# The bias rows leave SBUF once and are spread from memory to memory later

## The chip, the cores and the metric

The kernel runs on one core of one Trainium2 chip. The metric is the device time of one execution in microseconds; the time given is the median of several runs.

## The reference

Two blocks follow each other on one activation `x` of 256 tokens by 1024 channels, all float32. The first mixes with a gated linear recurrence and a 16-head forgetting attention, and has a gated feed-forward part. The second has two layers with SwiGLU parts, of which the last mixes with an 8-head attention (called "moba"). Only that attention uses the relative-position bias, a table of 32 buckets by 8 heads that is looked up by the distance of query and key:

```python
dist_own = qpos[:, None] - (j * MOBA_BLOCK + jnp.arange(MOBA_BLOCK))[None, :]
bias_own = rel_table[t5_bucket(dist_own)].transpose(2, 0, 1).astype(f32)
s_own = jnp.einsum('bhqd,bhpd->bhqp', qb, kown).astype(f32) * scale + bias_own
s_own = jnp.where(dist_own >= 0, s_own, -jnp.inf)
```

For one head the bias depends on the distance alone. So one row of 384 numbers (`EXT`) holds all that a head needs, and query p reads the same row, shifted by p places.

## The kernel before

**The stream of weights.** All weights are one stream of parts, each 128 x 1024 float32 (512 KB), in the order of the phases in `PHASES`: `xa`, `v`, `gates`, `ga`, `qk`, `sa`, `sb`, `pa`, `pb`, `wo` and so on. SyncE loads part c into `raw[c % 4]` as soon as VectorE has made `w_lo` of part c-4 (function `load`). ScalarE makes the rounded half `w_hi` (`hi`, four parts ahead of TensorE), VectorE the remainder `w_lo` (`lo`, three parts ahead), and TensorE multiplies each part as three products of 128 x 128 by 256 columns per block (L1291, L1292, L1293, or L1384 to L1386 for token tiles). A full part has eight blocks, 24 matmuls. Each engine runs its own list in program order; semaphores alone tie them.

**Phases around the change.** `v` (8 parts, token tiles; ScalarE evacuates in pairs in `token_pair`, L356) is followed by `gates`, the two sigmoid gates of the recurrence: 8 parts that hold 8 and 5 blocks in turn, 156 matmuls in all. Their weights are parts 18 to 25. ScalarE writes the gates with a sigmoid (L375) out of banks 4 to 7, and between two evacuations of `v` it does the exponentials and the logarithms of the forget gate (`exponentials`, `logarithms`), each with a table load. After `ga` come `qk`, `sa`, `sb`; at their end POOL multiplies the last product of the recurrence (L1185) and has then nothing to do until the `merged` tiles are complete (L1187), where it loads `x` again and the level masks.

**The bias rows.** TensorE makes `ext`, 8 rows of 384 (one a head, on partitions 0 to 7), early in the program. ScalarE copies them to SBUF, in `work` where the sigmoids later write. POOL sends them to the memory tensor `bias_rows`, 128 copies a head (L1155), and ScalarE waits for the end of that transfer, semaphore `ext_out` (named bias_rows_out), before its first sigmoid:

```python
act.wait_ge(ext_out, 16)
for n in range(8):
    multiplied(PART["gates"] + n)
```

Much later, behind the SwiGLU loop of the first layer, POOL reads them back with a step of 383 per partition (L1271), which gives each partition its shift; VectorE adds the mask to them.

Of the kernel before, what the change touches and what calls it, by code (L numbers as in the profile page):

```python
# [13 lines left out]
F32 = mybir.dt.float32  # L14
# [6 lines left out]
P = 128  # L21
# [7 lines left out]
H_MOBA, DH_MOBA = 8, 128  # L29
# [37 lines left out]
EXT = 3 * P  # L67
# [4 lines left out]

def build(nc, stream, par_d, x_d, wf_d, table_d, onehot_d, ident_d, mask_d, lmask_d, out_d):
    scr = nc.dram_tensor("bias_rows", [H_MOBA, P, EXT], F32, kind="Internal")
    with ExitStack() as ctx:
        def sb(name, shape, dt=F32):
            return ctx.enter_context(nc.sbuf_tensor(name, shape, dt))

        def sem(name):
            return ctx.enter_context(nc.semaphore(name))  # L80
# [22 lines left out]
        def flat(ap):  # L103

            return ap.rearrange("p u t -> p (u t)")
# [7 lines left out]
        ext = flat(F[0:H_MOBA, 60:62, :])[:, 0:EXT]  # L113
# [30 lines left out]
        def dcol(name, e):  # L144
# [11 lines left out]
        x_in = [sem(f"x_half_in{i}") for i in range(2)]  # L156
        par_in, wf_in, tab_in, cst_in, x_back, lm_in, bias_in = (
            sem(n) for n in ("par_in", "wf_in", "table_in", "const_in", "x_back", "lmask_in", "bias_in"))
        ext_out, out_done = sem("bias_rows_out"), sem("out_done")
        ones_ready = sem("ones_ready")  # L160
        sq_ready, stat_done, rms_ready, rstd_ready = (
            sem(n) for n in ("square_ready", "stat_done", "rms_ready", "rstd_ready"))
# [93 lines left out]
        def _(act):  # L256
# [104 lines left out]
            for n in range(0, C, 2):  # L361
# [3 lines left out]
                if n == 4:  # L365
                    logarithms()
                    A(touch, touch, ACT.Sigmoid)
            act.wait_ge(ext_out, 16)
            for n in range(8):
                multiplied(PART["gates"] + n)  # L370
                m, g = n // 4, n // 2 % 2
# [150 lines left out]
            for l in range(1, LEVELS + 1):  # L522
                e, n = EB[l % 2], 2 * (l - 1)
# [604 lines left out]
        def _(pool):  # L1128
# [20 lines left out]
            for t in range(R):  # L1149
# [2 lines left out]
                                ALU.subtract).then_inc(xcl_ready, 1)  # L1152
            pool.wait_ge(ext_ready, 1)

            pool.dma_start(bass.AP(tensor=scr, offset=0, ap=[[P * EXT, H_MOBA], [EXT, P], [1, EXT]]),  # L1155
                           ext.rearrange("h (o e) -> h o e", o=1).to_broadcast([H_MOBA, P, EXT])).then_inc(ext_out, 16)

            pool.wait_ge(cst_in, 32)
            g.tensor_copy(EYE_R, ident[0:H_FOX, 0:H_FOX]).then_inc(cum_split, 1)
# [19 lines left out]
            for t in range(R + 2):  # L1179
                if t < R:  # L1180
                    g.tensor_tensor(IG[:, t, :], IG[:, t, :], XC[:, t, :], ALU.mult).then_inc(b_done, 1)
                if t >= 2:
                    pool.wait_ge(scan_done, t - 1)
                    pool.wait_ge(gelu_done, 1)
                    g.tensor_tensor(GA[:, t - 2, :], GA[:, t - 2, :], XC[:, t - 2, :], ALU.mult).then_inc(ya_done, 1)  # L1185

            pool.wait_ge(merged, C)  # L1187
            pool.dma_start(X, x_d).then_inc(x_back, 16)
            pool.dma_start(LM, lmask_d).then_inc(lm_in, 16)
# [80 lines left out]
            for j, (a, e) in enumerate([(0, P), (P, EXT)]):  # L1270
                pool.dma_start(BIAS[:, :, a:e], bass.AP(tensor=scr, offset=255 - P * j,  # L1271
                               ap=[[EXT - 1, P], [P * EXT, H_MOBA], [1, e - a]])).then_inc(bias_in, 16)
# [495 lines left out]
```

## Time and profile before

| | |
|---|---|
| median of 3 runs | 1272.76 us (1271.36 to 1272.99) |
| the profiled execution's span | 1272.8 us |
| TensorE busy | 1222.9 us, 96% |
| VectorE, ScalarE, POOL busy | 69%, 53%, 33% |
| mean granted TensorE clock | 0.974 |
| slices with a granted clock of 0.7 | one, the third of 40 (64 to 95 us) |

The profiled execution has its own time, which is its span, 1272.8 us, and lies at the median of the runs. How to read it: TensorE has work for nearly the whole span, so what counts is where it stands still or runs at a lowered clock. The page's 40 slices show one place where the clock fell to 0.7, in the third slice, and it is there that one reads on.

### The profile page before, as it was taken

To read this page: it belongs to the slowest core of one execution; us is meant where nothing else is said; L and a number is where in the kernel's file an instruction comes from. 1 tells how busy PE (TensorE), PEld (TensorE's weight loads), DVE (VectorE), ACT (ScalarE), POOL (GpSimd) and SP (SyncE) were. 2 spreads that over 40 slices of the span, in tenths; PEclk is the share of its full clock that TensorE was granted. 3 is DMA by queue.
4 is the path that set the end of the run, shared out by engine and by line. 5 is a ranking of instruction groups with operands and counts; after the bars stand their busy time and mean duration, and the time that the engine had idled before them with its cause. 6 is when DMAs were issued, how large, how long until landed. Compare 5 with 4: busy or idle time off the path is not lost.

```text
span 1272.8 us, 26105 instructions
## 1 busy us (share of the span) xinstructions
PE 1222.9 (96%) x9746; PEld 1194.9 (94%) x9746; DVE 876.0 (69%) x1215; ACT 680.4 (53%) x1017; POOL 425.8 (33%) x425
## 2 busy tenths in 40 slices
PE   8959999999999999999989989999999999999997
PEld 8949988899989999998989989999999999999996
DVE  7817666596789999547878778555666777655653
ACT  6538744563557677445634345555445555555542
POOL 3206200060235555212055547444321005544421
PEclk9979999999999999999988889999999999999999
DMA  6556522356635655652623325565765545655662
GB/s 220 157 132 219 157 95 83 103 153 209 230 91 181 191 172 187 206 180 86 201 78 100 100 67 169 181 183 183 250 206 168 182 134 150 190 186 178 194 202 76
DMA packets 56535, 204.51 MB, mean 161 GB/s; under 512 B 6616, under 2 KB 6744, under 8 KB 56336
## 3 DMA queue, kind: packets, MB, share of 16 engines
q1 hardware_dynamic: 54288, 197.35, 49.7%
q0 software_dynamic: 1600, 5.10, 1.9%
q8 instruction: 52, 0.85, 0.3%
q10 hardware_dynamic: 576, 1.05, 0.2%
q14 instruction: 19, 0.16, 0.0%
HBM read 200.85 MB, written 2.62 MB: 160 GB/s over the span
## 4 chain that ended last, share of the span: by engine, by line
PE 84%; DVE 9%; DMA 3%; ACT 2%; issue 1%; DVEq 0%; SPq 0%; ACTq 0%
PE bank L1291 25%; PE bank L1292 24%; PE bank L1293 24%; DMA raw<-in_stream 3%; DVE w_lo L642 2%; PE bank L1546 2%; PE bank L1473 1%; PE bank L1384 1%; PE bank L1385 1%; PE bank L1386 1%; DVE work L982 1%; DVE h_lo L672 1%; DVE work L796 1%; PE bank L1475 1%; DVE work L696 1%
## 5 line engine op out<-in xcount | busy, mean ns | idle before, releaser
L642 DVE TENSOR_TENSOR w_lo<-raw,w_hi 128x1024 fp32r<-128x1024 f32 x374 | 489.3, 1317 | 181.4 <-ACT w_hi L265 180.5
L1291 PE MATMUL bank<-h_hi,w_hi 128*128 128x256 f32 x1888 | 543.8, 288 | 9.5 <-DVE h_lo L672 5.2
L1292 PE MATMUL bank<-h_lo,w_hi 128*128 128x256 f32 x1888 | 536.6, 284 | 0.0
L1293 PE MATMUL bank<-h_hi,w_lo 128*128 128x256 f32 x1888 | 536.4, 284 | 0.0
L265 ACT ACTIVATE w_hi<-raw 128x1024 fp32r<-128x1024 f32 x374 | 392.1, 1052 | 242.1 <-PE bank L1293 218.6
L1291 PEld LDWEIGHTS bank<-h_hi,w_hi 128*128 128x128 f32 x1888 | 364.7, 193 | 16.2 <-issue 7.6
L1292 PEld LDWEIGHTS bank<-h_lo,w_hi 128*128 128x128 f32 x1888 | 365.0, 193 | 0.3
L1293 PEld LDWEIGHTS bank<-h_hi,w_lo 128*128 128x128 f32 x1888 | 364.6, 193 | 0.0
L1291 PE MATMUL bank<-u_hi,w_hi 128*128 128x256 f32 x868 | 250.3, 288 | 19.1 <-DVE w_lo L642 13.2
L1292 PE MATMUL bank<-u_lo,w_hi 128*128 128x256 f32 x868 | 248.6, 286 | 0.0
L1293 PE MATMUL bank<-u_hi,w_lo 128*128 128x256 f32 x868 | 248.4, 286 | 0.0
L1291 PEld LDWEIGHTS bank<-u_hi,w_hi 128*128 128x128 f32 x868 | 169.5, 195 | 21.3 <-issue 11.1
L678 DVE TENSOR_TENSOR work<-bank,work 128x256 f32<-128x256 f32 x218 | 90.5, 420 | 123.4 <-PE bank L1293 119.3
L1292 PEld LDWEIGHTS bank<-u_lo,w_hi 128*128 128x128 f32 x868 | 169.7, 196 | 0.0
L1293 PEld LDWEIGHTS bank<-u_hi,w_lo 128*128 128x128 f32 x868 | 169.7, 195 | 0.0
L1220 POOL TENSOR_TENSOR work<-work 128x256 f32<-128x256 f32 x68 | 82.4, 1211 | 177.6 <-ACT work L569 118.9
L1203 POOL TENSOR_TENSOR work<-work 128x256 f32<-128x256 f32 x46 | 34.5, 750 | 135.3 <-DVE work L1056 79.6
L1225 POOL TENSOR_TENSOR u_lo<-work,u_hi 128x256 f32 x68 | 70.1, 1031 | 11.4 <-POOL u_hi L1223 11.4
L569 ACT ACTIVATE work<-work 128x256 f32<-128x256 f32 x44 | 18.4, 417 | 74.1 <-PE bank L1293 74.1
L1384 PE MATMUL bank<-w_hi,h_hi 128*128 128x256 f32 x192 | 56.9, 296 | 0.0
L1385 PE MATMUL bank<-w_hi,h_lo 128*128 128x256 f32 x192 | 56.1, 292 | 0.0
L1386 PE MATMUL bank<-w_lo,h_hi 128*128 128x256 f32 x192 | 55.9, 291 | 0.0
(223 smaller groups left out, 1299.7 us busy)
## 6 DMA issues: line engine op xcount, KB each, us to landing
raw<-in_stream SPq DMA_DIRECT2D x374, 512.0 KB, 3.7
bias_rows<-work POOLq DMA_DIRECT2D x1, 1536.0 KB, 35.5
work<-in_x_t SPq DMA_DIRECT2D x2, 512.0 KB, 6.3
work<-in_x_t POOLq DMA_DIRECT2D x1, 1024.0 KB, 6.6
work<-bias_rows POOLq DMA_DIRECT2D x1, 1024.0 KB, 10.9
out<-work ACTq DMA_DIRECT2D x4, 256.0 KB, 2.5
work<-in_lmask POOLq DMA_DIRECT2D x1, 512.0 KB, 7.9
work<-bias_rows POOLq DMA_DIRECT2D x1, 512.0 KB, 6.5
```

What stands on the lines that cost most here:

```text
L265: A(w_hi[:, slot, :], raw[:, slot, :], ACT.Copy).then_inc(hi_ready, 1)
L642: v.tensor_tensor(w_lo[:, slot, :], raw[:, slot, :], w_hi[:, slot, :].bitcast(F32), ALU.subtract).then_inc(lo_ready, 1)
L678: v.tensor_tensor(dst, out_of(t), RSTD, ALU.mult).then_inc(evacuated, 1)
L1203: chain.wait(g.tensor_tensor(SQT, src[:, c, :], src[:, c, :], ALU.mult))
L1220: g.tensor_tensor(PB[:, pair, :], GB[:, pair, :], YB[:, 2 * pair + 1, :], ALU.mult).then_inc(pair_free, 1)
L1225: g.tensor_tensor(dst_l, PB[:, pair:pair + 1, :], dst_h.bitcast(F32), ALU.subtract).then_inc(ul_ready, 1)
L1291: mm(out, w_hi[:, slot, s], r_hi, start=start, stop=False)
L1292: mm(out, w_hi[:, slot, s], r_lo, start=False, stop=False)
L1293: return mm(out, w_lo[:, slot, s], r_hi, start=False, stop=stop)
L1384: mm(out, h_hi[:, b, ts], w_hi[:, s0:s0 + 2, f], start=(b == 0), stop=False)
L1385: mm(out, h_lo[:, b, ts], w_hi[:, s0:s0 + 2, f], start=False, stop=False)
L1386: last = mm(out, h_hi[:, b, ts], w_lo[:, s0:s0 + 2, f], start=False, stop=(b == BLK - 1))
```

## The change

The transfer out of SBUF at L1155 writes one row a head into a new small memory tensor `bias_row` (8 x 384, 12 KB). ScalarE now waits for this transfer, by the new semaphore `row_out`, ahead of its first sigmoid. A second transfer on POOL's queue reads `bias_row` with a step of zero and writes the 128 copies a head into `bias_rows`; POOL issues it behind its last product of the recurrence. It has the old semaphore `ext_out`, for which POOL waits ahead of reading back.

```diff
     scr = nc.dram_tensor("bias_rows", [H_MOBA, P, EXT], F32, kind="Internal")
+    row = nc.dram_tensor("bias_row", [H_MOBA, EXT], F32, kind="Internal")
...
-        ext_out, out_done = sem("bias_rows_out"), sem("out_done")
+        row_out, ext_out, out_done = sem("bias_row_out"), sem("bias_rows_out"), sem("out_done")
...
-            act.wait_ge(ext_out, 16)
+            act.wait_ge(row_out, 16)
...
             pool.wait_ge(ext_ready, 1)
 
-            pool.dma_start(bass.AP(tensor=scr, offset=0, ap=[[P * EXT, H_MOBA], [EXT, P], [1, EXT]]),
-                           ext.rearrange("h (o e) -> h o e", o=1).to_broadcast([H_MOBA, P, EXT])).then_inc(ext_out, 16)
+            pool.dma_start(bass.AP(tensor=row, offset=0, ap=[[EXT, H_MOBA], [1, EXT]]), ext).then_inc(row_out, 16)
...
                     g.tensor_tensor(GA[:, t - 2, :], GA[:, t - 2, :], XC[:, t - 2, :], ALU.mult).then_inc(ya_done, 1)
 
+            pool.wait_ge(row_out, 16)
+            pool.dma_start(bass.AP(tensor=scr, offset=0, ap=[[P * EXT, H_MOBA], [EXT, P], [1, EXT]]),
+                           bass.AP(tensor=row, offset=0, ap=[[EXT, H_MOBA], [0, P], [1, EXT]])).then_inc(ext_out, 16)
             pool.wait_ge(merged, C)
             pool.dma_start(X, x_d).then_inc(x_back, 16)
```

POOL's list where the rows leave SBUF, before: the ten remainders of `xc`, the transfer, and the forget gate's sums.

```order
L1151 TENSOR_TENSOR u_lo<-work,u_hi 128x256 [waits xc_hi_ready] x10
L1155 DMA bias_rows<-work 1024x1x384 [waits bias_rows_ready]
L1159 CAST u_hi<-ident 16x16 [waits const_in]
L1161 CAST u_hi<-ncum 16x256 [waits cum_ready]
L1163 TENSOR_TENSOR u_lo<-ncum,u_hi 16x256 [waits cum_split]
```

The same place of the changed kernel:

```order
L1152 TENSOR_TENSOR u_lo<-work,u_hi 128x256 [waits xc_hi_ready] x10
L1156 DMA bias_row<-work 8x384 [waits bias_rows_ready]
L1159 CAST u_hi<-ident 16x16 [waits const_in]
L1161 CAST u_hi<-ncum 16x256 [waits cum_ready]
L1163 TENSOR_TENSOR u_lo<-ncum,u_hi 16x256 [waits cum_split]
```

The transfer keeps its place; of 1024 rows that it writes, 8 are left. POOL's list behind the last products of the recurrence, before:

```order
L1181 TENSOR_TENSOR work<-work 128x256
L1185 TENSOR_TENSOR work<-work 128x256 [waits gelu_done,scan_done] x3
L1188 DMA work<-in_x_t 128x2048 [waits merged]
L1189 DMA work<-in_lmask 128x1024
L1191 MEMSET work 128x2048 [waits merged_lo]
```

And in the changed kernel:

```order
L1181 TENSOR_TENSOR work<-work 128x256
L1185 TENSOR_TENSOR work<-work 128x256 [waits gelu_done,scan_done] x3
L1188 DMA bias_rows<-bias_row 1024x1x384 [waits bias_row_out]
L1191 DMA work<-in_x_t 128x2048 [waits merged]
L1192 DMA work<-in_lmask 128x1024
L1194 MEMSET work 128x2048 [waits merged_lo]
```

The 1024 rows are now written from here, ahead of POOL's wait for `merged`.

## Rows read from the trace of the kernel before

**Rows 1.** The page, part 4: the chain that ended last.

```profile
PE 84%; DVE 9%; DMA 3%; ACT 2%; issue 1%; DVEq 0%; SPq 0%; ACTq 0%
```

**Rows 2.** Stretches, busy us: PE, PEld, DVE, ACT, POOL; then clock, DMA share, GB/s.

```profile
47.14:70.27 23.13, 23.13 (x194) 23.09 (x192) 10.63 (x13) 11.19 (x23) 5.16 (x6) 1.00 0.63 135
70.27:81.10 10.83, 0.16 (x2) 0.00 (x0) 1.22 (x1) 1.06 (x1) 0.00 (x0) 0.66 0.57 109
81.10:88.00 6.90, 4.36 (x24) 4.18 (x24) 1.22 (x1) 2.34 (x2) 0.00 (x0) 0.75 0.63 131
88.00:97.92 9.92, 7.60 (x35) 7.34 (x36) 6.01 (x8) 8.33 (x15) 2.02 (x1) 0.51 0.62 217
98.00:109.79 11.79, 11.79 (x100) 11.66 (x99) 8.69 (x13) 9.40 (x18) 10.09 (x12) 1.00 0.58 180
```

**Rows 3.** Who waited for whom, 50 to 100 us.

```profile
ACT w_hi L265 <- DMA raw<-in_stream: 19.0, 2, 13.1
PE bank L1291 <- DVE w_lo L642: 13.2, 2, 10.7
```

**Rows 4.** The chain that ended last, 50 to 115 us.

```profile
57.62 27.99 DMA raw<-in_stream
```

**Rows 5.** Transfers by line, whole span: KB each, us to landing.

```profile
raw<-in_stream SPq DMA_DIRECT2D x374, 512.0 KB, 3.7
bias_rows<-work POOLq DMA_DIRECT2D x1, 1536.0 KB, 35.5
work<-in_onehot POOLq DMA_DIRECT2D x1, 48.0 KB, 5.1
```

**Rows 6.** DMA queues, 57 to 65 us: packets, MB, share of 16 engines.

```profile
DMA packets 323, 0.94 MB, mean 118 GB/s; under 512 B 107, under 2 KB 107, under 8 KB 322
...
q0 software_dynamic: 178, 0.40, 48.5%
q1 hardware_dynamic: 144, 0.52, 22.3%
```

**Rows 7.** The same view, 50 to 95 us.

```profile
q0 software_dynamic: 704, 1.58, 31.6%
```

**Rows 8.** The same view, 909 to 920 us (the rows read back).

```profile
q0 software_dynamic: 397, 1.50, 40.0%
```

**Rows 9.** The same view, 1268 to 1272.8 us (the output stored).

```profile
q10 hardware_dynamic: 576, 1.05, 60.6%
```

**Rows 10.** ScalarE in order of time, 40 to 125 us: start, us.

```profile
64.72 0.84 ACT L356 ACTIVATE work<-bank,derived 128x256 f32<-128x256 f32 x2
...
86.71 1.28 ACT L345 ACT_TABLE_LOAD   x1
...
89.94 0.82 ACT L356 ACTIVATE work<-bank,derived 128x256 f32<-128x256 f32 x2
90.65 2.00 ACT L265 ACTIVATE w_hi<-raw 128x1024 fp32r<-128x1024 f32 x2
92.54 1.20 ACT L375 ACTIVATE work<-bank,par 128x256 f32<-128x256 f32 x3
93.61 1.08 ACT L265 ACTIVATE w_hi<-raw 128x1024 fp32r<-128x1024 f32 x1
```

**Rows 11.** POOL in order of time.

```profile
53.95 1.10 POOL L1155 DMA_DIRECT2D bias_rows<-work  x1
...
276.91 0.83 POOL L1185 TENSOR_TENSOR work<-work 128x256 f32<-128x256 f32 x1 [1.76 <-DVE work L796]
335.82 0.59 POOL L1188 DMA_DIRECT2D work<-in_x_t  x1 [58.08 <-DVE work L895]
```

**Rows 12.** VectorE in order of time, 255 to 300 us.

```profile
278.28 1.21 DVE L642 TENSOR_TENSOR w_lo<-raw,w_hi 128x1024 fp32r<-128x1024 f32 x1
```

**Rows 13.** The chain that ended last, 270 to 380 us.

```profile
279.62 0.38 PE bank L1291
```

**Rows 14.** Transfers by line, 280 to 335 us.

```profile
raw<-in_stream SPq DMA_DIRECT2D x21, 512.0 KB, 4.3
```

## The prediction

> **What bounds the kernel now.** I read the page's chain first: 84% of it is TensorE [rows 1], so a change pays only where TensorE stands still or is slow. The clock in the 40 slices points to the third. Its stretches [rows 2] give the size: `v` keeps TensorE busy to 70.27 us, then come 10.83 us with 0.16 busy, then 17 us with gaps at a granted clock of 0.75 and 0.51, and from 98.00 the last gates run at full clock to 109.79. The waits of this place [rows 3] name the order: TensorE waited once for 10.7 us for `w_lo`, and ScalarE for 13.1 us for a part of the stream to land. The chain passes there through one load of 27.99 us from 57.62 [rows 4]; the median load takes 3.7 us [rows 5]. What delays it stands beside it: the bias rows are issued at 53.95 [rows 11] and land 35.5 us later [rows 5], at 89.5. From 57 to 65 us their queue (q0) holds 48.5% of 16 engines, 7.8 engines' worth, for 0.40 MB; the stream's queue (q1) has 22.3% [rows 6]. So eight engines are full with the bias rows, and a stream part needs all sixteen. It is not ScalarE's wait for `ext_out` that costs: its first sigmoid is at 92.54, 3 us after the rows landed and right behind the two `w_hi` of 90.65 [rows 10], which came late because their parts did.
>
> **What the first edit gives back.** `v` makes 8 x 24 = 192 matmuls in 23.13 us [rows 2], 0.1205 us each. The gates have 156, so 18.8 us at full clock; they end at 109.79, 39.5 us after `v`. At most 39.5 - 18.8 = **20.7 us** come back: some 16 us of standing still and 4 to 5 us of slow clock.
>
> Is it all of them? The new transfer moves 12 KB; the nearest row is the one-hot table, 48 KB in 5.1 us [rows 5], so it lands near 60 us, long before ScalarE asks for it. ScalarE's own order decides next. Its third pair of `v` starts at 64.72 and takes 0.71 to the next start (as 89.94 to 90.65); two `w_hi` take 1.89 (90.65 to 92.54), which needs parts 18 and 19 landed by 66, and they are issued near 57 at 4 us each; the logarithms with their two table loads take 3.23 (86.71 to 89.94); then another pair 0.71, two `w_hi` 1.89, three sigmoids 1.07 [rows 10]. The sum: 65.4, 67.3, 70.6, 71.3, 73.2, 74.3. TensorE can begin the gates at 70.27 (part 18's `w_lo` needs 66.4 plus 1.2 [rows 12]) and wants the bank of the first three gates back after 24 + 15 matmuls, at 75.0. Margin 0.7 us. From 98.00 on the same loop shows no gap [rows 2]. I take 0.3 us off for waits of the tight start: **20.4 us**. If this order were worse than I read it, TensorE would lose what ScalarE is late, at most the 3.2 us of the logarithms.
>
> **What the second edit costs.** POOL's last product is at 276.91 and its next task at 335.82 [rows 11]: the issue (1.10 us [rows 11]) and the satisfied wait for `row_out` have 58 us of room, and nothing queues behind them in that time. The read-back is 600 us later. What counts is again the stream, since 1.57 MB go out beside it. The stretch is a tight one: the recurrence has made VectorE late, and TensorE starts a part at 279.62 [rows 13] just after its `w_lo` of 278.28 + 1.21 [rows 12]. Call this part c (times as before; all lies 20.4 us earlier after). Part c+4 can only be issued then, 279.5. TensorE reaches it four parts on, at 279.6 + 4 x 2.89 = 291.2 (2.89 is a part of `v` [rows 2]), less 1.1 for `w_hi` and 1.2 for `w_lo`: it must land by 288.9, the next ones by 291.8, 294.7 and 297.6. That allows 9.4 us where a load takes 4.3 [rows 14].
>
> How the queues share an engine is in [rows 6]: q0 has 178 packets less the 107 small ones, 71; q1 has 144 on sixteen engines, 72 on the eight. They take turns, packet by packet, 5.6 KB against 4 KB. A load has 8 packets an engine, so it costs 8 turns, and 1.57 MB are 35 turns on each of eight engines. A turn is one stream packet (22.3% of 8 x 16 us over 144, 0.2 us) and one bias packet, d/35, where d is the engine time that the copy takes on each engine. The first load lands at about 281 + 8 turns, and so on.
>
> No row shows a copy from memory to memory, so d is bounded. Above: as before, 31.6% of 16 x 45 us [rows 7] = 228 us, over 8 engines 28.4 us. Below: the rows read back cost 40.0% of 16 x 11 us for 1.50 MB [rows 8], 70 us, which is 9.2 us each on eight for 1.57 MB. The store of the output, 1.05 MB in 60.6% of 16 x 4.8 us, 46.5 us [rows 9], gives 8.7. So writing memory is cheap, and reading memory is cheap in rows of 0.5 and 1 KB; the one thing that only the slow transfer does is to read eight partitions 128 times each. I therefore stand near the lower end and take 12 us, since source and target are now both memory.
>
> - d = 9.2: turn 0.46, 3.7 us a load, nothing is late.
> - d = 12: turn 0.54, 4.3 us; landings 285.3, 289.6, 294.0, 298.3; the last is 0.7 late. I take **0.5 us**.
> - d = 20: 6.2 us a load, the fourth 8 late; 1 to 2 more for the clock.
> - d = 28.4: 8.1 us a load, the fourth at 313.4, 16 late; with up to the 4.5 us of slow clock, 16 to 20.
>
> The sum: 1272.8 (the profiled execution's own time, equal to the median within 0.1) - 20.4 + 0.5 = 1252.9; I say **1252.8**.
>
> The Trainium skill, "SBUF — State Buffer", section "Door 1: The DMA port swizzle", says why the source might be the slow side: partitions 0 to 3 share one port and 4 to 7 another, 27.2 GB/s each. By that page the old transfer takes 1.57 MB / 54.4 GB/s = 28.9 us, an estimate that agrees with the 28.4 us of [rows 7]; by it a copy from memory escapes the limit. Against the change speaks "DMA: Bandwidth & Descriptors", "Why a DMA increments its semaphore by 16 and not by 1": the engine count must divide the slowest dimension of both sides, and eight heads are still outermost in the source. By it the copy holds eight engines, as [rows 6] shows for the old one, and the sum stays as it is; on sixteen the 0.5 us would be nothing.
>
> **The rivals.**
>
> A. *The copy is as slow as before, the stall only moves.* For it: same row size, same eight heads, same 1024 writes into memory, and a turn-taking that would hurt `pa` as it hurt the gates. Against it: [rows 8, 9]. d = 24 to 32 gives 1268 to 1276.
>
> B. *Half way*, d of 14 to 24, because each engine both reads and writes memory: 1254.5 to 1267.
>
> C. *Slower than before.* One mechanism: all eight engines read the same 12 KB of memory over and over, and this place serves them one after another. No row has a repeated read from memory, so nothing excludes it. At d = 45 a turn is 1.49 and a load 11.9 us; the fourth lands at 328.6, 31 late, plus 4.5 of clock: 1272.8 - 20.4 + 35 = 1288. It decides from d near 28, where the stall eats the 20.4.
>
> D. *The first gain is smaller*, since ScalarE's logarithms, or VectorE's sums of the forget gate behind them, take the place of the late part: with 8 us lost there, 1261. Against it: the margins above.
>
> **How the numbers follow.** My forecast (d up to 14): 0.66, by itself 1250.5 to 1254.5. B 0.14, A 0.08, C 0.07, D 0.05. The lower end is the lowest run, 1271.4, less 20.7. The range from 1250.5 to 1264 holds the forecast, D and most of B, 0.8 in all. A measurement here tells 0.2%, 2.5 us, from no change. Faster than 1270.2: forecast, B, D and a part of A, 0.88. Same 0.04, slower 0.08.
>
> **What would show it.** The load of 28 us is gone and the stream's loads from 50 to 90 us take 4 to 5 us; the granted clock is 1.00 from 47 to the end of the gates, which comes near 89 us. ScalarE's first sigmoid is near 73. The copy is issued near 257 and lands 15 to 20 us after; its queue's engine time is near 100 us. From 257 to 280 TensorE waits under 1 us for `w_lo`. I am wrong if the copy takes over 20 us to land and TensorE stands between 265 and 300, or if the gates still have a gap of over 1 us.

## The result, and the profile after

The changed kernel takes 1250.09 us (median of 4 runs, 1246.08 to 1250.33), the kernel before beside it 1272.06 us: a ratio of 0.9828, 95% interval 0.9816 to 0.9839. Two later comparisons of the same two programs gave 0.9852 (0.9835 to 0.9868) and 0.9840 (0.9816 to 0.9864). The gain is 18 to 22 us by the medians; in the first pair of profiles 20.65 us can be followed through the trace to the edits. The forecast of 1252.8 was 2.7 us too high, and the time lies 0.4 us below the lower end of the range, 1250.5.

The page of the changed kernel: the first row has the granted clock in 40 slices, the second the chain that ended last, the third the transfer that writes the bias rows.

```profile
PEclk9999999999999999999988989999999999999998
...
PE 87%; DVE 10%; ACT 2%; issue 1%; DMA 1%; DVEq 0%; SPq 0%; ACTq 0%
...
bias_rows<-bias_row POOLq DMA_DIRECT2D x1, 1536.0 KB, 15.1
```

The third slice is at 9 again, where it was at 7; the transfers' part of the chain went from 3% to 1% [rows 1], and the 1.5 MB now land in 15.1 us, not 35.5 [rows 5]. The two stretches that answer to [rows 2], `v` and the gates (columns as there):

```profile
47.14:69.99 22.85, 22.85 (x192) 22.85 (x192) 12.69 (x15) 15.58 (x29) 4.57 (x6) 1.00 0.55 176
69.99:89.50 19.51, 19.32 (x161) 19.10 (x160) 15.41 (x20) 17.01 (x32) 13.03 (x12) 1.00 0.58 201
```

Behind `v` there is no gap and no slow clock. The gates' 156 matmuls are over at 88.8. ScalarE in order of time, where the kernel before had a wait of 13 us [rows 3, 10]:

```profile
64.44 0.84 ACT L357 ACTIVATE work<-bank,derived 128x256 f32<-128x256 f32 x2
65.17 2.01 ACT L266 ACTIVATE w_hi<-raw 128x1024 fp32r<-128x1024 f32 x2
67.20 1.28 ACT L346 ACT_TABLE_LOAD   x1
...
70.43 0.82 ACT L357 ACTIVATE work<-bank,derived 128x256 f32<-128x256 f32 x2
71.14 2.00 ACT L266 ACTIVATE w_hi<-raw 128x1024 fp32r<-128x1024 f32 x2
73.14 1.21 ACT L376 ACTIVATE work<-bank,par 128x256 f32<-128x256 f32 x3
74.23 1.06 ACT L266 ACTIVATE w_hi<-raw 128x1024 fp32r<-128x1024 f32 x1
```

The order is the one that the prediction laid out: ScalarE goes on from the first three sigmoids at 74.2, and the prediction had 74.3. The issue of the copy, at 257.1 us, and the stretches around it:

```profile
L1188 POOL DMA_DIRECT2D bias_rows<-bias_row x1: 1169/1169/1169, 257.1 to 257.1; - x1
```

```profile
255.00:260.00 5.00, 4.72 (x37) 4.32 (x37) 4.96 (x9) 3.56 (x8) 1.96 (x2) 1.00 0.49 130
260.00:265.00 5.00, 5.00 (x44) 5.00 (x43) 4.97 (x9) 3.92 (x8) 0.00 (x0) 1.00 0.80 291
265.00:270.00 5.00, 5.00 (x44) 5.00 (x44) 1.42 (x2) 1.61 (x3) 0.00 (x0) 1.00 0.80 313
270.00:275.00 5.00, 5.00 (x44) 5.00 (x43) 3.08 (x5) 3.32 (x4) 0.00 (x0) 1.00 0.82 298
```

TensorE's busy time, the number behind the length of the stretch, is 5.00 of 5 us from 260 us on, while the transfers move up to 313 GB/s. The 4.72 us before that are not the copy's doing: the kernel before has the same 4.72 at the same place of its program (275 to 280 us). What the copy's queue takes, 250 to 300 us:

```profile
q1 hardware_dynamic: 2603, 9.46, 56.4%
q0 software_dynamic: 704, 1.58, 8.4%
```

704 packets and 1.58 MB as in [rows 7], but 8.4% of 16 x 50 us, 67 us of engine time in sum, where the transfer out of SBUF took 228.

To see where the two profiles part, I read in both the start of VectorE's `w_lo` for the first part of each phase. The difference (before less after) is 0.3 us at `xa`, 13.5 at `gates`, 20.2 at `ga`, 20.65 at `qk`, and it stays 20.6 to 20.7 through `pa`, where the copy is, and on to `hg`. Then it becomes 19.4 at `ho` and 24.6 at `up1`, and is 24.6 at the end. So the first edit gives 20.65, the second costs nothing, and 3.9 us come from a place that no edit touches. It is also the place where the page of the kernel before has four slices of 8 in its granted clock, 636 to 764 us.

### The profile page after: what moved, and what is told of

Read it like the earlier page. It is cut to its first block, busy times and chain, and to the rows that moved or that the text cites. A ratio compares the mean times of both kernels' runs of the same rounds, so it can differ in the third digit from the quotient of the medians.

```text
span 1248.2 us, 26106 instructions
## 1 busy us (share of the span) xinstructions
PE 1213.8 (97%) x9746; PEld 1186.6 (95%) x9746; DVE 878.6 (70%) x1215; ACT 680.8 (55%) x1017; POOL 427.8 (34%) x426
## 4 chain that ended last, share of the span: by engine, by line
PE 87%; DVE 10%; ACT 2%; issue 1%; DMA 1%; DVEq 0%; SPq 0%; ACTq 0%
PE bank L1294 25%; PE bank L1295 25%; PE bank L1296 25%; DVE w_lo L643 2%; PE bank L1549 2%; PE bank L1387 1%; PE bank L1389 1%; PE bank L1388 1%; PE bank L1476 1%; DVE h_lo L673 1%; DVE work L983 1%; DVE work L797 1%; PE bank L1478 1%; DVE work L697 1%; DVE work L976 1%
## 5 line engine op out<-in xcount | busy, mean ns | idle before, releaser
L1294 PE MATMUL bank<-h_hi,w_hi 128*128 128x256 f32 x1888 | 543.3, 288 | 10.5 <-DVE h_lo L673 6.1
## 6 DMA issues: line engine op xcount, KB each, us to landing
bias_rows<-bias_row POOLq DMA_DIRECT2D x1, 1536.0 KB, 15.1
```

What stands on the lines that cost most here:

```text
L1294: mm(out, w_hi[:, slot, s], r_hi, start=start, stop=False)
```

## The experiments

**The two programs once more**, unchanged.

> The kernel before, unchanged, profiled once more. The changed kernel's profile is 24.6 us shorter, of which 20.65 lie ahead of the first matmuls of qk and 3.9 between the last level products and the second layer's feed-forward part (19.44 saved when ho begins, 24.58 when up1 begins), a place that the edit does not touch. Theory chance: in that place the granted clock falls for a while in each execution, and how long varies from one to the next; this profile then may have the time of either, and the difference of the medians stays near 22. Theory shift: the earlier start moves the dips of the clock for good; this profile then repeats the first one's times there (716.7 at ho, 770.2 at up1, 53.5 us between them) within 0.3 us.

> The changed kernel, unchanged, profiled once more. Chance: the time from ho to up1 (48.3 us in its first profile) is different from it by over 1 us in this one or in that of before. Shift: 48.3 us within 0.3 again. Either way the gates end within 0.3 us of 89.5, and nothing is lost where the copy runs. Time 1246 to 1251.

Before: 1271.34 us (10 runs, 1269.79 to 1274.55), 1.0003 (0.9993 to 1.0012) of before. After: 1252.84 us (4 runs, 1250.16 to 1253.81). The stretch from `hg` to `up1` in the four profiles, in the order before, its repeat, after, its repeat (clock third from the end):

```profile
677.44:770.15 92.71, 84.40 (x622) 81.89 (x622) 70.73 (x77) 38.85 (x51) 46.67 (x32) 0.89 0.29 87
```

```profile
678.84:767.85 89.01, 81.58 (x622) 79.18 (x622) 73.55 (x77) 38.73 (x51) 45.72 (x32) 0.92 0.29 90
```

```profile
656.75:745.57 88.82, 81.62 (x622) 79.23 (x622) 73.77 (x76) 38.70 (x51) 45.69 (x32) 0.92 0.29 90
```

```profile
656.66:749.42 92.76, 84.32 (x622) 81.83 (x622) 70.72 (x77) 38.77 (x51) 46.65 (x32) 0.89 0.29 87
```

The same 622 matmuls take 89 or 92.8 us in either program, with a mean granted clock of 0.92 or 0.89. Before happened to have the long case in its first profile and after the short one; in the repeats it was the other way round. A fixed shift falls, chance stands. Looked at more closely, what differs is a number of dips, stretches of some 7 us at a granted clock of 0.50. The long profile of before has three, of which these are the inner parts:

```profile
678.00:684.00 6.00, 6.00 (x29) 6.00 (x29) 5.71 (x4) 0.74 (x1) 3.84 (x2) 0.50 0.53 175
723.00:729.00 6.00, 6.00 (x30) 6.00 (x30) 0.98 (x2) 1.12 (x1) 1.82 (x1) 0.50 0.20 72
747.00:753.00 6.00, 4.87 (x21) 4.57 (x22) 4.64 (x6) 1.52 (x3) 1.65 (x3) 0.50 0.21 57
```

Its repeat has two, with full clock between them:

```profile
691.00:697.00 6.00, 6.00 (x30) 6.00 (x30) 4.63 (x3) 0.00 (x0) 4.58 (x2) 0.50 0.55 178
699.00:743.00 44.00, 39.72 (x328) 38.25 (x327) 37.08 (x38) 21.89 (x29) 23.69 (x17) 1.00 0.28 84
746.00:752.00 6.00, 5.92 (x29) 5.92 (x30) 2.73 (x4) 1.06 (x1) 0.00 (x0) 0.53 0.38 105
```

After has two in its first profile and three in its repeat. In these two pairs one dip more goes with 3.7 and 3.9 us.

At `qk` the repeats stand at 132.47 and 110.98, 21.5 apart. The gates of after ended where they were expected; the loss in the gates of before varies from execution to execution (28.3 or 28.6 us for `gates`, 23.6 or 24.5 for `ga`). The repeat of after missed its expected time: 1252.84 us, where 1246 to 1251 had been given.

**Does ScalarE's wait cost?**

```diff
-        ext = flat(F[0:H_MOBA, 60:62, :])[:, 0:EXT]
+        ext = sb("ext_own", [P, EXT])[0:H_MOBA, :]
...
-            act.wait_ge(ext_out, 16)
```

> The kernel before, but the bias rows stand in a tile of their own and ScalarE does not wait for their transfer; the transfer itself is as it was. Theory source (a transfer out of eight partitions fills eight engines for 28 us each and starves the stream): unchanged, 1271 to 1273, a load of some 28 us and 10 us without matmuls after v. Theory wait (what cost was ScalarE's wait ahead of its first sigmoid): 1250 to 1253.

1270.91 us (10 runs, 1269.52 to 1273.81), a ratio of 1.0001 (0.9991 to 1.0011). The chain between 50 and 110 us:

```profile
57.19 27.17 DMA raw<-in_stream
84.39 1.06 ACT w_hi L265
```

Without the wait the load is as long [rows 4] and so is the time. The wait cost nothing that can be seen beside an interval of 0.1%.

**Place or source?** The old transfer, out of the same eight partitions, at the place of the copy: the tile and the missing wait of the experiment above, and

```diff
-            pool.dma_start(bass.AP(tensor=scr, offset=0, ap=[[P * EXT, H_MOBA], [EXT, P], [1, EXT]]),
-                           ext.rearrange("h (o e) -> h o e", o=1).to_broadcast([H_MOBA, P, EXT])).then_inc(ext_out, 16)
...
+            pool.dma_start(bass.AP(tensor=scr, offset=0, ap=[[P * EXT, H_MOBA], [EXT, P], [1, EXT]]),
+                           ext.rearrange("h (o e) -> h o e", o=1).to_broadcast([H_MOBA, P, EXT])).then_inc(ext_out, 16)
             pool.wait_ge(merged, C)
```

> The bias rows stay in a tile of their own, ScalarE does not wait, and the old transfer out of eight partitions is issued where the changed kernel issues its copy. Theory source: q0 again 28 us of each of eight engines, landing after 35 us, loads of 8 us in pa, TensorE stands about 16 us between 265 and 300 with some slow clock: 16 to 20 us above the changed kernel, 1266 to 1270. Theory place (what helped was to move the transfer to a stretch with room for it): TensorE waits under 2 us, 1250 to 1252.

1268.04 us (10 runs, 1263.67 to 1273.5), ratio 0.9981 (0.9965 to 0.9997). The queue from 250 to 310 us, TensorE's wait and two of its stretches:

```profile
q0 software_dynamic: 704, 1.58, 23.0%
```

```profile
PE bank L1289 <- DVE w_lo L641: 14.9, 3, 11.8
```

```profile
275.00:280.00 5.00, 0.00 (x0) 0.00 (x0) 0.00 (x0) 0.50 (x1) 0.00 (x0) 0.50 0.51 90
280.00:285.00 5.00, 2.73 (x13) 2.73 (x13) 1.23 (x1) 0.96 (x2) 0.00 (x0) 0.50 0.65 130
```

23.0% of 16 x 60 us over eight engines are 27.6 us each, as in [rows 7], and TensorE stands and slows in `pa`, to a granted clock of 0.50, as it had in the gates. From the first part of `pa` to that of `wo` this program takes 64.4 us, the changed kernel 46.9: 17.5 us, of the 16 to 20 that the prediction gave rival A. Place alone is worth 2.4 us by the ratio, 0.4 to 4.5 by its interval, and the ten executions spread over 10 us.

The prediction's model, in which the two queues take turns packet by packet, had the size but not the order. It serves the loads one behind the other, 8 us each. In the trace the four loads issued from 258.8 to 267.8 us are in flight together and take 20.7, 25.3, 27.5 and 24.5 us. The first two of them:

```profile
raw<-in_stream SPq DMA_DIRECT2D x1, 512.0 KB, 20.7
```

```profile
raw<-in_stream SPq DMA_DIRECT2D x1, 512.0 KB, 25.3
```

The first lands at 279.4 us, 12 later than by turns; the last lands at 292.3, and turns give 258.8 + 4 x 8.1 = 291.2.

The other half of the cross, the copy from memory at the early place:

```diff
             pool.dma_start(bass.AP(tensor=row, offset=0, ap=[[EXT, H_MOBA], [1, EXT]]), ext).then_inc(row_out, 16)
+            pool.wait_ge(row_out, 16)
+            pool.dma_start(bass.AP(tensor=scr, offset=0, ap=[[P * EXT, H_MOBA], [EXT, P], [1, EXT]]),
+                           bass.AP(tensor=row, offset=0, ap=[[EXT, H_MOBA], [0, P], [1, EXT]])).then_inc(ext_out, 16)
```

> The changed kernel with its copy from memory to memory issued at once, behind the transfer of the eight rows, near 57 us, into the tight stretch of v and the gates. Theory source: engine time near 67 us over eight engines as in the changed kernel's first profile, landing after 15 us; two or three loads take 6 to 9 us, which the ring takes up: TensorE stands under 2 us, time within 2 us of the changed kernel. Theory place: most of the 20 us come back, 1265 to 1272.

1249.94 us (4 runs, 1246.55 to 1250.62), ratio 0.9831 (0.9810 to 0.9851). Its queue takes 9.1% of 16 x 45 us, 8.2 us of each of eight engines, the copy lands in 14.7 us, the three loads it slows most take 7.4, 8.5 and 5.2 us, and `qk` begins at 110.81, where the changed kernel has 111.11. The tight stretch bears it without loss. So the gain is the source's: the copy gives all of it at either place, the old source almost none.

**What is slow in the source?** The eight rows on partitions 0, 4, 8 to 28, everything else as before:

```diff
-        ext = flat(F[0:H_MOBA, 60:62, :])[:, 0:EXT]
-        table = F[0:BUCKETS, 46, 0:H_MOBA]
+        ext32 = flat(F[0:4 * H_MOBA, 60:62, :])[:, 0:EXT]
+        ext = bass.AP(tensor=ext32.tensor, offset=ext32.offset, ap=[[4 * ext32.ap[0][0], H_MOBA], [0, P], [1, EXT]])
+        table = F[0:BUCKETS, 46, 0:4 * H_MOBA]
...
+    table4 = np.zeros((BUCKETS, 4 * H_MOBA), np.float32)
+    table4[:, ::4] = a["rel_bias_table_2"]
```

> The kernel before with the eight rows on partitions 0, 4, 8 to 28 in place of 0 to 7 (the table is padded with zero columns, so that each head comes out four partitions apart); same place, same bytes, same row size, same wait. The old transfer moved 1.57 MB in 28.4 us of each of eight engines, 55 GB/s in all. Theory ports (partitions 0 to 3 and 4 to 7 share one way out each): eight ways now, q0 takes 8 to 11 us of each engine, it lands in 14 to 20 us, and the time is that of the changed kernel within 3 us. Theory partition (an engine is slow because it reads one partition again and again): nothing changes, 35 us to landing, 1270 to 1273.

The transfer's source and ScalarE's and TensorE's write of the rows change to match and are left out here. And on partitions 0, 2, 4 to 14, the same edit with 2 in place of 4:

> As eight_ports, but with the rows on partitions 0, 2, 4 to 14: two rows on each of four ways out. Theory ports: 1.57 MB over four ways of the rate seen for two (27.7 GB/s each) are 14.2 us; q0 has 14 to 16 us of each of eight engines, it lands in 18 to 23 us, loads of 5 to 6 us, TensorE loses 0 to 5 us against eight_ports: 1250 to 1257. Theory neighbours (any two rows further apart than one partition are read at full rate): as eight_ports, 9 us of each engine and 14.4 us to landing.

In both programs ScalarE still waits for `ext_out`, as in the kernel before. The queue from 50 to 95 us and the landing, first with the rows on every fourth partition, then on every second:

```profile
q0 software_dynamic: 704, 1.58, 10.0%
...
bias_rows<-work POOLq DMA_DIRECT2D x1, 1536.0 KB, 14.4
```

```profile
q0 software_dynamic: 704, 1.58, 13.7%
...
bias_rows<-work POOLq DMA_DIRECT2D x1, 1536.0 KB, 18.2
```

Per engine (share x 16 x 45 us / 8): 28.4 us with partitions 0 to 7 [rows 7], 12.3 with every second, 9.0 with every fourth; 35.5, 18.2 and 14.4 us to landing. The time falls with it, 1270 to 1273, then 1257.21 (0.9895, 0.9878 to 0.9911), then 1250.92 (0.9836, 0.9817 to 0.9856). In all three the same eight rows are each read 128 times, so the repeated reading is not what is slow; it is that the rows are neighbours.

The order of the three fits the Trainium skill ("SBUF — State Buffer", "Door 1: The DMA port swizzle"), by which partitions 0 to 3 share one port, and 4 to 7 the next: two, four and eight ports. The size does not quite: by the engine time, a port gave 27.6 GB/s when there were two and 31.9 when there were four, where the expectation had the same for both. No run holds the distance of the rows and changes only the port, so the port as the cause stays an inference.

The case of every second partition took less of each engine, 12.3 us, than the 14 to 16 expected, and yet cost 3.9 us against every fourth between `v` and `qk`. Its four loads issued from 56.3 to 63.2 us take 10.5 to 12.8 us and not the 5 to 6 expected; with every fourth partition the same four take 6.9 to 9.8. The chain from 60 to 90 us, and TensorE's stretch behind `v`:

```profile
57.46 12.82 DMA raw<-in_stream
```

```profile
75.00:80.00 5.00, 1.44 (x7) 1.47 (x8) 3.42 (x6) 5.00 (x11) 0.00 (x0) 0.83 0.31 107
```

Part 19, which this load brings, makes ScalarE late for its logarithms, its first sigmoid starts at 77.2, and TensorE waits 3.6 us for the bank. The bias rows had landed by then, 18.2 us after 53.8, so it is the load and not the wait for `ext_out`. The rest of the 6.3 us between the medians is the stretch behind `hg` (91.9 us with three dips, and 88.9, in the two profiles).

**How much room has the place?** The copy four times, the three more written as a loop here:

```diff
+            for k in range(3):
+                pool.dma_start(bass.AP(tensor=spare, offset=k * H_MOBA * P * EXT, ap=[[P * EXT, H_MOBA], [EXT, P], [1, EXT]]),
+                               bass.AP(tensor=row, offset=0, ap=[[EXT, H_MOBA], [0, P], [1, EXT]])).then_inc(spare_out, 16)
```

> The changed kernel with the copy made four times, into four tensors, one behind the other on the queue (three are extra work). This measures how much room the place has. Turn model: each copy 35 turns on eight engines, a turn near 0.44 us, 62 us in all; a load costs 8 turns, 3.5 us, where TensorE takes 2.9, so the stream falls 0.6 us behind a load, less the 5.6 us of room: 5 us lost, 1253 to 1258. If copies and loads share the engines without taking turns (the copies take what is left), nothing is lost, 1249 to 1251. If the copies come first, 15 us or more are lost.

1252.78 us (0.9853, 0.9836 to 0.9871). The median is just below the 1253 to 1258 expected. From `pa` to `wo` it takes 50.1 us, 3.2 more than the changed kernel; the model of turns said 5. Two of its stretches, and TensorE's wait:

```profile
265.00:275.00 10.00, 9.99 (x83) 9.79 (x83) 2.78 (x3) 2.74 (x4) 0.00 (x0) 1.00 1.00 364
275.00:285.00 10.00, 9.25 (x77) 9.04 (x76) 5.91 (x7) 4.02 (x4) 0.00 (x0) 1.00 1.03 381
```

```profile
PE bank L1303 <- DVE w_lo L645: 2.5, 2, 1.7
```

With 4.7 MB more than needed, the engines are full at 364 to 381 GB/s and the stream falls behind by only 2.5 us of waits.

**Sixteen engines for the copy**: in the early copy, 128 outermost on both sides (only the `ap` part of each line is shown).

```diff
-                           ap=[[P * EXT, H_MOBA], [EXT, P], [1, EXT]]
-                           ap=[[EXT, H_MOBA], [0, P], [1, EXT]]
+                           ap=[[EXT, P], [P * EXT, H_MOBA], [1, EXT]]
+                           ap=[[0, P], [EXT, H_MOBA], [1, EXT]]
```

> As early_copy, but the copy is written with 128 outermost on both sides and the heads inside, so that its engine count is not bounded by eight heads. If the outermost count decides: all sixteen engines, engine time in sum as before (67 us, 4.2 each), landing in 8 to 10 us, time within 1 us of early_copy. If not: 15 us to landing.

It lands in 11.2 us, not 14.7, with 10.0% of the engines' time (72 us in sum, 4.5 each if it is on sixteen); 1251.22 us (0.9854, 0.9832 to 0.9875), not distinct from early_copy. The landing lies between the two expectations, nearer to that for sixteen engines; the views do not show engines one by one, so the count itself stays inferred.

**The stretch behind `hg`.** Both programs a third time, and the changed kernel with matmuls of no use in TensorE's waits:

> The changed kernel once more. What is asked is the stretch from the first part of hg to the first of up1, which no edit touches: it took 92.8 us in the first profiles of before and of the repeat of the changed kernel, and 88.8 to 89.1 in eight others. Theory chance: 89 or 92.8 again, everything else as before to 0.3 us; the median lies between 1249 and 1253.5, the two medians had so far. Theory fixed shift is already without support.

> The kernel before once more, beside after_third on the same chip, for the difference of the two: 20.3 to 20.7 us by the stretches up to qk, and by the medians 18 to 22.5. The stretch from hg to up1 takes 89 or 92.8 us.

```diff
+            def keep_in_gap(n, t):
+                free_bank(0, 0, t)
+                for _ in range(n):
+                    mm(bank[t % BANKS][:, S:S + P], ones[:, :], ones[:, :], start=True, stop=True)
...
+                        if c == PART["ho"] and b >= 4:
+                            keep_in_gap(3, t + 1)
...
+                        keep_in_gap(16, TILE["hi"] + 1)
                         pe.wait_ge(k_ready, C)
...
+                keep_in_gap(4, TILE["hi"] + n + (2 if l < LEVELS else 1))
                 pe.wait_ge(x_low, l)
```

> The changed kernel with 60 matmuls that compute nothing of use put ahead of TensorE's waits in the level products (16, then 4 a level) and in the first tile of ho (12), the places where it stands for 0.6 to 4.5 us between hi and up1. Theory clock (that stretch varies by 3.9 us, and loses more always, since the granted clock falls to half there): the granted clock stays at 1.00 in most of it, the time from hi to up1 falls from 136.2 by 3 to 10 us and is the same in each execution; total 1241 to 1248. Theory waits (the 3.9 us are waits for VectorE or POOL): no gain, or 1 to 3 us of loss by the added matmuls.

After: 1251.46 us (1246.77 to 1252.57), before 1270.35 (1269.27 to 1272.14). At `qk` they stand at 111.11 and 130.44, only 19.3 apart where 20.3 to 20.7 had been expected, so the loss of the old transfer varies by 2 us (20.65, 21.5, 19.3). The stretch behind `hg` was 88.9 us with two dips in before and 91.4 with three in after. All profiles without added matmuls fit this: nine with two dips take 88.8 to 89.1 us, four with three dips 91.4 to 92.8. From `hi` to `up1`, changed kernel and then with the added matmuls:

```profile
609.43:745.57 136.14, 123.04 (x928) 119.95 (x927) 113.80 (x106) 58.66 (x74) 68.34 (x39) 0.91 0.30 94
```

```profile
609.19:738.67 129.48, 125.41 (x1048) 123.04 (x1047) 110.40 (x106) 58.76 (x74) 69.49 (x39) 1.00 0.31 99
```

(The trace has two records for each of the 60 matmuls added, 1048 less 928.) The clock is 1.00, no dip is left, and the stretch is 6.7 us shorter than in a profile with two dips behind `hg`. The four runs lie between 1242.87 and 1244.27, median 1243.05 (0.9789, 0.9773 to 0.9805). The theory of waits falls. This version beats both kernels; what it adds has nothing to do with the bias rows.

## Why the prediction came out as it did

- **What bounds**: right. The chain's load of 28 us was the transfer's doing; with it gone, the loads between 50 and 90 us take 3.4 to 5.0 us. The wait for `ext_out` was rightly set aside (no_act_wait, 1.0001).
- **The first edit**: "at most 20.7 us come back" was right, 20.65 at `qk`. The 0.3 us for the tight start were not needed; ScalarE was done with the first three sigmoids 0.1 us from the time worked out.
- **The second edit**: the choice of d = 12 us was mis-sized. It is 8.4 us, below even the lower bounds of 9.2 and 8.7, and the queue's engine time is 67 us, not near 100. By the prediction's own list nothing is late then, and nothing was: cost 0, not 0.5. The reason for standing near the lower end, that only the read of eight partitions is slow, was right, and the two-port estimate beside it (28.9 us) was borne out by the size of the old transfer, 28.4 us of each engine.
- **The turns**: the model in which copy and load take turns packet by packet was wrong in its order. At d = 28.4 it gives 8.1 us to each load, one behind the other, but [rows 4] already has a load of 27.99. In the kernel before, the four loads issued from 56.5 to 65.9 us take 22.2 to 28.0 us at the same time. Beside the copy of the changed kernel, too, the four loads issued from 259.0 to 265.0 take 7.8 to 9.2 us, not 4.3. They land at 266.8, 269.8, 272.3 and 273.4, and the prediction's own limits, moved forward by 20.6 us, are 268.3, 271.2, 274.1 and 277.0: none is late, but the first two have only some 1.4 us left. The model spread the stream's 144 packets evenly over sixteen engines; no view shows engines one by one, so which part of it failed stays open.
- **Rivals**: A (as slow as before) would have come true with the old source, 1268.04 measured against 1268 to 1276; C, slow reads of the same 12 KB from memory, did not happen, and four copies in a row did not bring it about. B and D had no part in the changed kernel; what D describes, late logarithms of ScalarE, is what cost the 3.6 us in four_ports.
- **The step that failed**: the first term of the sum, "1272.8 (the profiled execution's own time, equal to the median within 0.1)", and with it the lower end, "the lowest run, 1271.4, less 20.7". 1272.8 is the span of the trace. The later profiles have a time 1.8 us above their span (1272.26 and 1270.4; 1249.96 and 1248.2), which puts that execution at 1274.6, above all of the runs given; that the span lay at their median was a coincidence. The execution was also a long one, with three dips behind `hg`, where the first profile of after had two, worth 3.9 us that the sum had no term for. Net, the start was 2.1 us too high for an execution with two dips. With the 0.3 and the 0.5 that were not needed, this is the difference between forecast and result (2.7 us) within 0.2.
- **The lower end** was wrongly added, too: 1271.4 less 20.7 is 1250.7, not 1250.5. It took the scatter of three runs for all of it. Over 25 runs of one comparison the kernel before spreads from 1268.92 to 1274.01. The changed kernel's twelve executions fall into three groups by the mean granted clock of the whole run: 1246.1 to 1246.8 us at 0.988 to 0.990, 1250.0 to 1250.6 at 0.985, and 1252.3 to 1253.8 at 0.981 or 0.982. The profiles with two dips behind `hg` and with three are in the second and the third group; that the first has one dip less still is likely but no trace shows it. A median of four such runs lies where most of them happen to fall: 1250.09 here, 1252.84 and 1251.46 in the repeats, both inside the range. The lower end had the whole 20.7 us and no cost of the copy in it, so the 0.4 us by which the range was missed are not the bias rows' doing, and to meet it would have been luck as well.

## What to carry to other kernels

A transfer of little data can stop a stream of much: look at how many engines' worth its queue fills, and for how long, before its place or its wait. Here a source of eight neighbouring partitions, read many times, was best sent out once and spread from memory. Laid on partitions four apart it gave the same time within the noise for no extra transfer (1250.92 us, though `qk` began 1.1 us later in its profile). And read the scatter of the runs, and the stretch in which it arises, before a range is drawn to a fraction of a microsecond; begin a sum with a time, not with the span of a trace.

## What the runs showed of the hardware that was not expected

- The read of eight neighbouring partitions is the limit, not the eight engines' worth of queue time: by that time, 1.57 MB in 28.4 us (55 GB/s) from partitions 0 to 7, in 12.3 us (128 GB/s) from every second, in 9.0 us (175 GB/s) from every fourth.
- A slow transfer on some of the engines holds back every load of the stream that is in flight beside it. In the kernel before, four loads issued within 10 us took 22.2 to 28.0 us each, where the median load takes 3.7, and the first of them landed 22.2 us after its issue.
- A copy from memory to memory with the same eight rows read 128 times each costs an engine no more than a plain read-back: 67 us of engine time for 1.57 MB, against 70 us for 1.50 MB in [rows 8].
- In a stretch where TensorE waits often, for 0.7 to 4.5 us, the granted clock falls to half for some 7 us at a time, twice in some executions and three times in others of the same program: 88.8 to 89.1 us or 91.4 to 92.8 us for the same 622 matmuls. Sixty matmuls in those waits held the clock at 1.00, gave 6.7 us back and narrowed four runs to 1.4 us.
